# Decode attention: key pages grouped by heads and turned in 32x32 blocks on VectorE, two score sets, scaling on GpSimd, output slab split at column 192

## The reference

```python
k_p, v_p = cache_k[page_table], cache_v[page_table]    # 8 sequences x 8 pages x 128 tokens x 16 heads x 64
f_past = lf_p - cumsum(lf_p, reverse=True)
s = einsum('bqhd,bkhd->bhqk', q, k_all) / 8 + f_q - f_key
s = where(k_pos <= q_pos, s, -inf)
p = softmax(s)
o = einsum('bhqk,bkhd->bqhd', p, v_all)
h = h + o.reshape(B, T, D) @ fox_w_o
```

## Time and profile before

| what | value |
|---|---|
| time, median of 3 runs | 1601.19 us (1600.58 to 1601.4) |
| profiled execution, its own time | 1601.69 us |
| its span | 1600.1 us |
| TensorE busy | 1563.8 us (98%) |
| VectorE busy | 974.6 us (61%) |
| ScalarE busy | 688.5 us (43%) |
| GpSimd busy | 95.8 us (6%) |
| moved by DMA | 255.02 MB, mean 159 GB/s |

### The profile page before, as it was taken

How to read it: one execution, slowest core, us unless ns; L and a number is a source line. 1 busy time by engine, 2 the same in 40 slices (tenths; PEclk the granted TensorE clock), 3 DMA queues, 4 the chain that set the end, 5 groups by cost and what they waited for, 6 DMA issues and landing times.

```text
span 1600.1 us, 34795 instructions
## 1 busy us (share of the span) xinstructions
PE 1563.8 (98%) x14400; PEld 1472.0 (92%) x14400; DVE 974.6 (61%) x1539; ACT 688.5 (43%) x1048; POOL 95.8 (6%) x129
## 2 busy tenths in 40 slices
PE   7999999998999999999999999999999999999998
PEld 7999997997888899999999999999777769999998
DVE  6655437686896575554458555545767766655532
ACT  4443324563655553333353434333355544433421
POOL 0000000002322200000001430000000000000000
PEclk9999998999999999999999999999999999999999
DMA  7444452430100554444445454446779993444442
GB/s 234 159 151 139 143 174 77 139 126 16 30 17 10 160 184 140 148 151 145 152 132 193 146 162 156 132 156 231 247 292 388 373 339 111 154 138 155 151 146 79
DMA packets 207199, 255.02 MB, mean 159 GB/s; under 512 B 17858, under 2 KB 188114, under 8 KB 206946
## 3 DMA queue, kind: packets, MB, share of 16 engines
q1 hardware_dynamic: 203426, 247.64, 46.0%
q0 software_dynamic: 3648, 5.57, 1.4%
HBM read 246.84 MB, written 6.35 MB: 158 GB/s over the span
## 4 chain that ended last, share of the span: by engine, by line
PE 90%; DVE 6%; ACT 2%; DMA 1%; issue 1%; SPq 0%; DVEq 0%
PE ps L723 23%; PE ps L724 23%; PE ps L725 23%; PE ps L1018 4%; PE ps L1013 3%; PE ps L1359 3%; PE ps L1448 2%; PE ps L775 1%; DVE ring_r L2035 1%; PE ps L1044 1%; PE ps L1443 1%; PE ps L1153 1%; PE ps L1169 1%; PE ps L1108 1%; DMA ring<-in_ffn_w_in 1%
## 5 line engine op out<-in xcount | busy, mean ns | idle before, releaser
L723 PE MATMUL ps<-arena_r,ring_r 128*128 128x320 f32 (+1 forms) x2016 | 625.8, 310 | 0.1
L725 PE MATMUL ps<-arena_r,ring_r 128*128 128x320 f32 (+1 forms) x2016 | 623.2, 309 | 0.0
L2035 DVE TENSOR_TENSOR ring_r<-ring,ring_r 128x2048 fp32r<-128x2048 f32 (+1 forms) x130 | 291.3, 2242 | 252.7 <-ACT ring_r L1565 147.4
L723 PEld LDWEIGHTS ps<-arena_r,ring_r 128*128 128x128 f32 x2016 | 379.9, 188 | 4.0 <-issue 3.0
L725 PEld LDWEIGHTS ps<-arena_r,ring_r 128*128 128x128 f32 x2016 | 379.9, 188 | 0.0
L724 PE MATMUL ps<-arena_r,ring_r 128*128 128x320 f32 x1136 | 351.0, 309 | 0.0
L724 PE MATMUL ps<-xn_r,ring_r 128*128 128x320 f32 (+2 forms) x880 | 272.3, 309 | 0.0
L724 PEld LDWEIGHTS ps<-arena_r,ring_r 128*128 128x128 f32 x1136 | 213.3, 188 | 0.2
L2035 DVE TENSOR_TENSOR arena_r<-arena,arena_r (+3 forms) x155 | 141.9, 926 | 111.7 <-ACT arena_r L1565 49.6
L1565 ACT ACTIVATE ring_r<-ring 128x2048 fp32r<-128x2048 f32 (+1 forms) x70 | 128.3, 1834 | 128.5 <-DMA ring<-in_ffn_w_out 89.4
L723 PE MATMUL ps<-arena_r 128*128 128x320 f32 x592 | 183.2, 309 | 0.0
(11 more groups left out here) (365 smaller groups left out, 1879.2 us busy)
## 6 DMA issues: line engine op xcount, KB each, us to landing
ring<-in_ffn_w_in SPq DMA_DIRECT2D x67, 1024.0 KB, 5.0
arena<-in_cache_v SPq DMA_DIRECT2D x64, 512.0 KB, 6.5
ring<-in_cache_k SPq DMA_DIRECT2D x64, 512.0 KB, 5.9
ring<-in_ffn_w_out SPq DMA_DIRECT2D x24, 1024.0 KB, 5.1
arena<-in_ffn_w_in SPq DMA_DIRECT2D x21, 1024.0 KB, 5.0
ring<-in_rw_w_rkv SPq DMA_DIRECT2D x11, 1024.0 KB, 5.2
ring<-in_ffn_w_out SPq DMA_DIRECT2D x12, 768.0 KB, 4.4
arena<-in_ffn_w_out SPq DMA_DIRECT2D x8, 1024.0 KB, 5.1
```

What stands on the lines that cost most here:

```text
L723: pe.matmul(out, part(s, 1)[:, k, cs], x_hi, start=first_, stop=False)
L725: return pe.matmul(out, part(s, 0)[:, k, cs], x_hi, start=False, stop=last)
L2035: return TT(out, x, high.bitcast(F32), ALU.subtract)
```

## The change

Key pages are loaded with heads in groups of four: partition 32g+u gets, for tokens 4u to 4u+3, the 256 floats of head group g. VectorE turns them in place of TensorE, one instruction a page, in blocks of 32x32, from the ring straight into `k_feat`, which then holds on 32 partitions a half of a head's features for each of the four groups. Value pages are loaded with token 4u+f on partition 32f+u, to match. The order of heads and tokens changes accordingly in the constants (`later`, `selcol`), in the forget terms (`past_copies`), in the queries (now a product with a 0/1 mask of four groups, on GpSimd) and in the samples' own keys and queries, which TensorE regroups in two new tiles (`k_own`, `q_own`, `head_groups`). The scores get two sets of banks, used in turn. The scaling of the prompt heads' probabilities and most of `out_low` go to GpSimd; `fox_out`, `output_columns` and the copies to `p_T` go to ScalarE. `first_outputs` splits its columns at 192 instead of 256. The order of the loop is rewritten on all engines.

```diff
@@ constants
-    m["later"] = i[:, None] > i[None, :]
+    m["later"] = i[:, None] > (i % 32 * 4 + i // 32)[None, :]
@@ load_k, load_v (SyncE)
-                sp.dma_start(k_page(b, j), A["cache_k"][bass.ds(page_of(b, j), 1)].rearrange("a t h d -> (a t) (h d)")
+                page = A["cache_k"][bass.ds(page_of(b, j), 1)].rearrange("a t h d -> (a t) (h d)")
+                sp.dma_start(k_page(b, j).rearrange("p (f x) -> p f x", f=4), page.rearrange("t (g x) -> g t x", g=4)
                              ).then_inc(k_page_in(b, j)[0], 16)
...
-                sp.dma_start(v_page(j), A["cache_v"][bass.ds(page_of(b, j), 1)].rearrange("a t h d -> (a t) (h d)")
-                             ).then_inc(S(f"v_page{j}"), 16)
+                page = A["cache_v"][bass.ds(page_of(b, j), 1)].rearrange("a t h d -> (a t) (h d)")
+                sp.dma_start(v_page(j), page.rearrange("(u f) x -> f u x", f=4)).then_inc(S(f"v_page{j}"), 16)
@@ TensorE
-            def turn_page(b, j):
-                turn_half(b, j, 0)
-                turn_half(b, j, 1)
+            def head_groups(name, src):
+                t = first[name]
+                begin(t)
+                out = bank(t).rearrange("p (c x t) -> p c x t", c=2, x=4)
+                for x in range(4):
+                    for g in range(4):
+                        r = slice(32 * g, 32 * g + 32)
+                        mm = mmul(out[r, :, x, :], ident[:, 32 * x:32 * x + 32], src[:, 2 * g:2 * g + 2, TP:T])
+                end(mm)
...
             def unit_scores(b, u):
                 if u == 0:
-                    pe.wait_ge(S("q_cur"), b * 4 + 4)
+                    pe.wait_ge(S("q_cur"), b + 1)
                 if u % 2 == 0:
                     pe.wait_ge(S("nfk_rep"), 2 * b + u // 2 + 1)
-                    if b:
-                        pe.wait_ge(S("p_row"), (b - 1) * 3 + u // 2 + 1)
-                turn_evicted(b, 2 * u + 1)
-                bk, c0 = SCORES[u // 2], u % 2 * 256
+                    if b > 1:
+                        pe.wait_ge(S("p_row"), (b - 2) * 3 + u // 2 + 1)
+                        pe.wait_ge(*((S("pT_ready"), 3 * (b - 1)) if u else (S("o_out"), 2 * (b - 1))))
+                pe.wait_ge(S("page_turned"), b * PAGES + 2 * u + 2)
+                bk, c0 = SCORES[b % 2][u // 2], u % 2 * 256
...
             for b in range(BS):
                 last = b == BS - 1
-                if b:
-                    turn_page(b, 1)
                 fox_scores(2 * b)
...
+                unit_scores(b, 1)
                 fox_scores(2 * b + 1)
-                unit_scores(b, 1).then_inc(S("half_scored"), 1)
                 if b:
                     for j in range(4):
                         page_outputs(b - 1, j)
-                turn_page(b, 4)
-                turn_page(b, 5)
...
-            first_outputs(0, slice(0, TP))
+            first_outputs(0, slice(0, T - P))
             turn_output(b)
-            first_outputs(1, slice(0, TP))
+            first_outputs(1, slice(0, T - P))
@@ VectorE
-            def page_copy(b, j):
-                dve.wait_ge(S("page_turned"), b * PAGES + j + 1)
-                CP(k_feat[j // 2 % 2][:, 4:8, j % 2 * P:(j % 2 + 1) * P],
-                   ps[:, turn_bank(b, j, 1), :].rearrange("p (m t) -> p m t", m=4)).then_inc(S("turned_dve"), 1)
+            def turn_page(b, j):
+                unit = (b * PAGES + j) // 2
+                if unit >= 2:
+                    dve.wait_ge(S("unit_scored"), unit - 1)
+                dve.wait_ge(*k_page_in(b, j))
+                dve.transpose(k_feat[unit % 2][:, j % 2 * D:(j % 2 + 1) * D], k_page(b, j)).then_inc(S("page_turned"), 1)
...
             for b in range(BS):
                 last = b == BS - 1
...
+                turn_page(b, 2)
+                turn_page(b, 3)
                 fox_scored(2 * b)
...
+                turn_page(b, 4)
+                turn_page(b, 5)
+                fox_scored(2 * b + 1)
+                fox_sums(2 * b)
+                turn_page(b, 6)
+                turn_page(b, 7)
+                fox_sums(2 * b + 1)
+                half_max(b)
                 if b:
                     probability_sums(b - 1)
+                    scaled_output(b - 1)
...
+                less_max(b)
                 if not last:
+                    turn_page(b + 1, 0)
+                    turn_page(b + 1, 1)
@@ GpSimd
+            def probabilities(hd):
+                s, st = s_pr[hd % 2], fstat[:, hd % 2, :]
+                pool.wait_ge(S("fox_sums"), hd + 1)
+                pool.tensor_tensor(s[:, 0:P], s[:, 0:P], st[:, 8:9].to_broadcast([P, P]), ALU.mult)
+                pool.tensor_tensor(s[:, P:3 * P], s[:, P:3 * P], st[:, 9:10].to_broadcast([P, 2 * P]), ALU.mult
+                                   ).then_inc(S("p_ready"), 1)
...
+            for b in range(BS):
+                if b + 1 < BS:
+                    queries(b + 1)
+                probabilities(2 * b)
+                probabilities(2 * b + 1)
+                if b + 1 < BS:
+                    out_low(b)
```

More of the change, by code:

```diff
@@ L511, in build @@
                 n_join += 1
[L513 to L531, removed]
+        out_bank = first["fo"] % 8
+        SCORES = [[(out_bank + 2 * j + n) % 8 for n in range(2)] for j in range(2)]
+        FOX, OUT = (out_bank + 4) % 8, (out_bank + 5) % 8
+        P_TURNED = [(out_bank + n) % 8 for n in (6, 7)]
+        OWN = P_TURNED[1]
         def states_stored(eng):
@@ L1387, in _ @@
-            act_done(first["q_norm"])
-            turn_half(0, 1, 1)
-            head_rep("q_rep", rs, lambda: turn_evicted(0, 1), 2)
+                        mm = pe.transpose(ps[:, P_TURNED[half], m * P:(m + 1) * P], p_row[:, c:c + P], ident)
+                    mm.then_inc(S("p_turned"), 1)
+                pe.wait_ge(S("p_row"), b * 3 + 3)
+                pe.transpose(ps[0:TS, SCORES[b % 2][1], 0:P], p_row[:, PAST:PAST + TS], ident).then_inc(S("p_turned"), 1)
+            head_groups("k_own", kT)
@@ L1391, in fox_scores @@
+            head_totals("q_norm", q_sq, S("q_sq"), 2)
+            head_rep("q_rep", rs, parts=2)
+            dve_done(first["q_rep"] + DT - 1)
+            head_groups("q_own", q_f)
             def fox_scores(hd):
@@ L1497, in _ @@
                         page_outputs(b - 1, j)
-                turn_page(b, 4)
-                turn_page(b, 5)
-                if not last:
-                    fox_turn(2 * b)
-                turn_page(b, 6)
                 unit_scores(b, 2)
@@ L1506, in _ @@
                         page_outputs(b - 1, j)
-                turn_page(b, 7)
+                if not last:
+                    fox_turn(2 * b)
+                unit_scores(b, 3)
+                own_scores(b)
                 if not last:
                     fox_turn(2 * b + 1)
-                    turn_page(b + 1, 0)
                     fox_values(b)
-                if b and not last:
+                if b:
                     turn_output(b - 1)
-                unit_scores(b, 3)
-                own_scores(b)
             b = BS - 1
-            turn_output(b - 1)
             fox_turn(2 * b)
@@ L1882, in _, with head_roots @@
             ffn(1)
-            def head_roots(name, src_name, src, dst, sq_sem, norm_name, ahead=4, out=None):
+            def head_roots(name, src_name, src, dst, sq_sem, norm_name, ahead=4, out=None, before_root=None):
                 for q in range(4):
@@ L1929, in probability_copy @@
             def probability_copy(b):
-                act.wait_ge(S("p_turned"), b + 1)
-                act.activation(p_T[:, 0:4, :], ps[:, turn_bank(b, PAGES, 0), :].rearrange("p (g c) -> p g c", g=4),
-                               ACT.Copy).then_inc(S("turned_act"), 1)
+                if b:
+                    act.wait_ge(S("outputs_done"), b)
+                for half in range(2):
+                    act.wait_ge(S("p_turned"), 3 * b + half + 1)
+                    act.activation(p_T[:, 4 * half:4 * half + 4, :],
+                                   ps[:, P_TURNED[half], :].rearrange("p (g c) -> p g c", g=4), ACT.Copy
+                                   ).then_inc(S("pT_ready"), 1)
+                act.wait_ge(S("p_turned"), 3 * b + 3)
+                act.activation(p_T[0:TS, 8, :], ps[0:TS, SCORES[b % 2][1], 0:P], ACT.Copy).then_inc(S("pT_ready"), 1)
             def fox_columns(hd):
```

276 lines of the change are left out of this document (107 added, 169 removed).

## The result

The changed kernel takes **2076.15 us** (median of 4 runs, 2075.15 to 2078.09) against 1601.3 (1600.58 to 1601.86) before: ratio 1.296, 95% interval 1.294 to 1.298. The forecast was 2068, with a range of 1990 to 2150.

A forecast was written before the change was run, and what follows sets the result against it. TensorE set the pace with DMA close behind; the change makes page loads, on four engines, the bound. Loads from about 1106, 676 + 5.4 + 1 us, end at 1788; plus 279.6, -1 and 1.6: 2068 us, range 1990 to 2150.

The forecast's parts named there:

- Four outermost entries, four engines: Page loads: a source with four outermost entries is carried by four DMA engines, twelve idle; 84 in 100.
- The nearest row, the eight-row store: Store of the sample's shift rows: 32 KB went as 8 packets of 4 KB, so at most eight engines carried it.
- 102.5 and 96.3 GB/s, last value page in at 1788 us: Page loads: quarter rates for value and key pages, 5.1 and 5.45 us each, 676 us together from about 1106.
- The output slabs: Two slabs issued within the last sequence put 65.5 KB on each engine at 24.1 GB/s, 5.4 us together.
- The 1 us for the last receipt: End of the page loads: 1 us added for the last receipt before the last value page is in.
- Nothing idle between the loads: SyncE's in-order page loads: longest chain of waits has eight loads, 42 us, still queued, so the four engines stay full.
- The tail, 279.6 - 1 us: After the last value page: 279.6 us follow as before, the output slab changing that by -1 (-3 to +4.5).
- The other edits lie under the loads: Attention stage: TensorE, VectorE, GpSimd and ScalarE changes all lie under a sequence's 84 us of page loads.
- The rival on the other side, 16 engines and 1577 us: All 16 engines carry the pages at 397 GB/s, last page at 1297, 1577 us, faster; 9 in 100.
- the ring of waits: Chain from landed value page through outputs, scaled_output and turn to the next key load; judged covered by queued loads, 42 us.
- The rival with one kind of page, 1822 us: Only one kind of page falls to four engines: 349 plus 82 us, last page near 1543; 4 in 100.

The follow-up runs named there:

- both_rows: Changed kernel with key and value pages both read as 128 whole rows, every other edit kept: 1598.53 us, ratio 0.999.
- before_v4: Kernel before the change, with only the value pages' source read in four outer stretches: 1843.16 us in one run.
- outer8: Changed kernel with both kinds of page read in eight outer stretches of 16 rows: 1727.9 us in one run.
- v_rows: Changed kernel with only the value pages read as 128 whole rows again, key pages left at four outermost entries: 1871.47 us, ratio 1.168.
- outer16: Changed kernel with both kinds of page read in 16 outer stretches of 8 rows: 1670.71 us, ratio 1.043.
- k_quarters: Changed kernel, tokens in their own order, each key page in four loads of 32 partitions, value pages as whole rows in one load: 1673.47 us, ratio 1.047.
- both_rows_early: Changed kernel, both kinds of page read as whole rows, two of VectorE's next-sequence page turns moved ahead of scaled_output(b-1): 1584.72 us, ratio 0.991.
- outer32: Changed kernel with both kinds of page read in 32 outer stretches of 4 rows: 1607.28 us in one run.
- both_rows_256: Changed kernel with both kinds of page read as whole rows and first_outputs split at column 256 again: 1602.27 us, ratio 1.002.
- before_192: Kernel before the change, with only the output slab's columns split at 192 in place of 256: 1597.95 us, ratio 0.998.

## Why the prediction was right, step by step

- **Four outermost entries, four engines.** Right, and shown: undone, the loss is gone (both_rows), put alone into the old kernel it is there (before_v4), and four packets are in progress at a time. The nearest row, the eight-row store, went over GpSimd's queue; it pointed the right way for SyncE's too, for eight (outer8, share 0.51) and for four.
- **102.5 and 96.3 GB/s, last value page in at 1788 us.** Measured 97 to 105 GB/s from 1200 to 1700 us, and 1789.5. Counted by packets, a key page took 5.42 us (5.45 forecast) and a value page 5.0 (5.1), so the 128 pages make 667 us instead of 676. The output slabs took the difference back: the last 99 us up to 1789 held 16.8 value pages, 84 us, so about 15 us went to the slabs, of which two were counted, at 5.4. Three were issued, and a 4 KB packet beside them took 206 to 236 ns in the mean (5 us from 1705, 1725 and 1775) instead of 160. That the page came within 1.5 us is in part luck: two errors of some 10 us cancelled. The 1 us for the last receipt stood on no row; the last data packet ended at 1789.0, 0.5 before its products began.
- **Nothing idle between the loads.** Right: SyncE waits 1.9 us in all before its page loads. What was not foreseen is that a load waits inside its issue as well; it still lands late, the last value load, issued at 1765.1, 24 us later. SyncE's two groups after:

```profile
L653 SPq DMA_DIRECT2D arena<-in_cache_v x64: 601/7136/13581, 1102.9 to 1765.1; - x64
```
```profile
L645 SPq DMA_DIRECT2D ring<-in_cache_k x64: 602/618/12398, 1125.5 to 1677.1; - x64
```

  (nanoseconds: shortest, median, longest). Only the output slabs stood between them, and none of those came late for TensorE, so no cost of the held issues is seen.
- **The tail, 279.6 - 1 us.** This term was mis-sized: 287.0 were measured (2076.5 - 1789.5). The output slab was taken to start at half clock and to rise within it; the clock stayed at 0.50 to 1810 us and was 0.59 in the next 10. So the term came out at +7.4, above even its upper end of +4.5. Up to the last of the 96 products it is +6.8: the last outputs took 2.0 us at half clock instead of 1, and the products 21.4 instead of at most 20.4. The next slab adds 0.6: 18 of its products ran at half clock, 13 before. The 8.4 us by which -1 missed, with the 1.5 by which the last page came later, are the whole distance from 2068 to the profiled execution's 2078.09.
- **The other edits lie under the loads.** Right. A turn takes 1.23 us (1.1 estimated), a 128x256 product on GpSimd 0.61 (0.90), neither seen in the time. The clock was 0.56 in the mean from 1200 to 1700 us, and TensorE's work still fit (busy 142 of these 500 us).
- **The rival on the other side, 16 engines and 1577 us.** Its condition does not hold. Its price was mis-sized as well: it let the loads run at 397 GB/s without a stop. both_rows shows 354 and 1598.5; the ring of waits that the prediction ruled out because 42 us of loads would be queued holds them up once the loads are fast, since by its own sum the queue then drains in a quarter of the time. With two turns moved it is 1584.7.
- **The rival with one kind of page, 1822 us.** v_rows made it real: 1871. Its sum, 6.7 us a pair, took both kinds at the rate that each has alone; side by side a pair took 7.65.
- **What would have been needed.** The grouping by heads needs a different head group on each quarter of the partitions; it was tried with four outermost entries and with four loads a page. Whether one load can be written with more outermost entries on both sides and the same places was not tried. Four loads cost SyncE's queue 3.7 to 6.2 us a pair of pages, where before needed 22.2/8 = 2.8. All three ways of it stay 4.7% or more above before. Whether four loads shared between two issuing engines would do was not tried.

## What to carry to other kernels

When a load's access pattern is rearranged, look at its outermost count on both sides before anything else: with 4 and 8 it used that many engines here, and the DMA share of the stretch showed it at once (0.27, 0.51). Then count issues: splitting the loads to spread them moved the bound to the issuing queue. Then look at what full engines carry, since the same share stood beside 384 and 241 GB/s. And when an engine is relieved, look for the ring of waits through the written order of the others: here a single wait ahead of the page turns took back 14 us of what the lighter TensorE had offered.

## What the runs showed of the hardware that was not expected

- All engines busy does not mean full rate: 259 GB/s at share 1.03 (outer16) and 241 at 1.09 (k_quarters), against 384 at 0.99 (both_rows_early). The order of the rows or pieces differs (in k_quarters also their size), and it shows in the single packet: 4 KB in 256 ns against 159, 1 KB in 79 against 46. In k_quarters the whole-row loads beside the key quarters are slowed as well (261 ns). Why 64 KB between an engine's rows is slow (outer16) and 128 KB is not (outer32), while 128 KB between the pieces of a partition is slow again (k_quarters), stays open.
- A load's issue on SyncE took 0.33 us for 128 whole rows, 0.32 or 0.56 for quarters, 0.60 at least with four outermost entries, and up to 13.6 us when the engines behind it were full. Which load is held then does not go by its own pattern: in v_rows it was the whole-row value loads (median 4.7 us), in before_v4 the whole-row key loads (3.5).
- Score products that read neighbouring columns 1 KB apart took 2.19 us for 16 instructions against 1.07.
- The granted clock fell to 1.2 GHz with TensorE fully busy, in the output slab's second range of 64 columns (0.53 from 1334 us in before, 0.67 and 0.50 in both_rows_256), and not in one of 128 (1.00 in before_192 and both_rows). After the mostly idle stage it stayed at 1.2 GHz through products of 192 and 128 columns and into the 320-column ones behind them (0.50 from 1790 to 1810 us, 0.59 in the next 10), TensorE busy 10.0 of every 10 us.
